# Hybrid decoder layer on 8 cores: where the first pieces, the row terms, the last quarter of x and the output blocks are loaded

## The reference

```python
proj = x @ w_in                       # 2048 x 10280: q, k, v, forget logits, z_att, z_ssd, xBC, dt
# 8 attention heads of 128: causal softmax(q k / sqrt(128) + F[t] - F[s]) v, F = cumsum(log sigmoid(f))
att = fox_attention(q, k, v, log_f) * silu(z_att)
# Mamba-2: conv of 4 taps and silu on xBC, 32 heads of 64 in 8 groups, chunks of 128
y = ssd_chunked(xs, dt, A, B, C) + d_skip * xs
y = gated_group_rmsnorm(y, z_ssd, ssd_norm_w)
x = layer_norm(2 ** 0.25 * x + concat([att, y]) @ w_out, ln_g, ln_b)
```

## Time and profile before

| | |
|---|---|
| Median of 3 runs | 1677.75 us |
| Profiled execution | 1675.15 us |
| Its span on the slowest core (core 1) | 1673.6 us |
| Spans of the 8 cores | 1664.3 to 1673.6 us |
| PE busy | 1635.6 us (98%) |
| DVE, POOL, ACT busy | 1135.5, 883.6, 849.6 us |
| DMA | 191.33 MB, mean 114 GB/s |

### The profile page before, as it was taken

The page is one execution under the profiler, slowest core; times in us unless marked ns, Lnnn a source line. Parts: engine busy times, 40 slices in busy tenths (PEclk is TensorE's granted clock), DMA queues, the critical chain, the costliest instruction groups (busy, mean ns, idle before and its releaser), DMA issues.

```text
span 1673.6 us, 31910 instructions; the slowest of 8 cores (1664.3 to 1673.6 us)
## 1 busy us (share of the span) xinstructions
PE 1635.6 (98%) x9108; PEld 801.4 (48%) x9108; DVE 1135.5 (68%) x2342; ACT 849.6 (51%) x1979; POOL 883.6 (53%) x1377
## 2 busy tenths in 40 slices
PE   5999999999999999999999999999999999999997
PEld 2454544544555455445554455455545544444443
DVE  2676777767876887678668876777778666444444
ACT  2767665665665666666666666666566610000000
POOL 2164564655664667468556765656567523222221
PEclk9999999999999999999999999999999999999999
DMA  9955954593457345644652473239556776445431
GB/s 169 149 79 92 134 97 93 114 123 91 104 103 131 81 92 110 112 97 85 126 87 73 89 139 64 54 77 157 110 112 126 197 194 189 138 139 139 139 95 76
DMA packets 180538, 191.33 MB, mean 114 GB/s; under 512 B 118828, under 2 KB 137132, under 8 KB 175980
## 3 DMA queue, kind: packets, MB, share of 16 engines
q1 hardware_dynamic: 164348, 126.89, 31.4%
q0 software_dynamic: 16016, 62.40, 23.5%
HBM read 198.74 MB, written 39.85 MB: 143 GB/s over the span
## 4 chain that ended last, share of the span: by engine, by line
PE 92%; DMA 4%; issue 1%; DVE 1%; ACT 1%; SPq 0%; POOL 0%; another core or an unknown queue 0%; DVEq 0%; ACTq 0%; POOLq 0%
PE bank L544 91%; DMA mixd<-att 1%; DMA xq<-xT 1%; DMA rowb<-arowd 1%; DMA mixd<-yn 1%; DMA xtok<-xsf 0%; SPq L603 0%; DVE xt L577 0%; PE bank L833 0%; ACT L555 0%; SPq L605 0%; PE bank L762 0%; ACT u L555 0%; ACT dec L555 0%; DVE acc L577 0%
## 5 line engine op out<-in xcount | busy, mean ns | idle before, releaser
L544 PE MATMUL bank<-xq,slab 128*128 128x512 bf16 x3072 | 726.0, 380 | 0.0
L544 PE MATMUL bank<-slab,xq 128*128 128x512 bf16 x2048 | 480.7, 379 | 1.1 <-DMA slab<-wpack 1.1
L544 PEld LDWEIGHTS bank<-xq,slab 128*128 128x128 bf16 x3072 | 293.9, 98 | 304.9 <-issue 3.9
L577 DVE SCALAR_TENSOR_TENSOR acc<-u,cst,acc 128x512 f32<-128x512 f32 x384 | 328.1, 857 | 51.5 <-ACT acc L555 38.8
L544 PEld LDWEIGHTS bank<-slab,xq 128*128 128x128 bf16 x2048 | 197.2, 98 | 211.4 <-issue 1.5
L555 ACT ACTIVATE dec<-rowb,nb 128x128 bf16<-128x128 f32 x512 | 202.2, 397 | 28.1 <-PE bank L544 16.2
L555 ACT ACTIVATE P<-bank,boff 128x512 bf16<-128x512 f32 x192 | 131.1, 683 | 68.7 <-PE bank L544 67.8
L544 PE MATMUL bank<-wo,mTa 128*128 128x512 bf16 x704 | 163.7, 379 | 0.0
L555 ACT ACT_TABLE_LOAD x14 | 18.0, 1283 | 273.6 <-DVE st L1169 270.3
L577 DVE SCALAR_TENSOR_TENSOR xt<-xt,bank 128x512 f32<-128x512 f32 x64 | 43.9, 685 | 141.1 <-PE bank L544 140.8
L566 POOL TENSOR_TENSOR xdd<-xtok,dtde 128x256 bf16<-128x256 bf16 x120 | 83.1, 692 | 85.3 <-PE bank L544 62.9
(11 more groups left out here) (113 smaller groups left out, 2197.8 us busy)
## 6 DMA issues: line engine op xcount, KB each, us to landing
slab<-wpack POOLq DMA_DIRECT2D x80, 512.0 KB, 8.7
rowb<-arowd SPq DMA_DIRECT2D x128, 256.0 KB, 4.0
xt<-x_tok SPq DMA_DIRECT2D x16, 1024.0 KB, 5.0
out<-xt SPq DMA_DIRECT2D x15, 1024.0 KB, 4.3
gbc<-growd SPq DMA_DIRECT2D x32, 256.0 KB, 5.2
mixd<-yn SPq DMA_DIRECT2D x128, 64.0 KB, 2.3
xq<-xT POOLq DMA_DIRECT2D x15, 512.0 KB, 33.8
wo<-w_out POOLq DMA_DIRECT2D x11, 512.0 KB, 9.6
```

The lines of the kernel that those rows point to most:

```text
L544: fns.append(lambda e, o=o, a=a, b=b, s=s, t=t: e.matmul(o, a, b, start=s, stop=t))
L577: return p.op("dve", [lambda e: e.scalar_tensor_tensor(out=o, in0=a, scalar=s, in1=b, op0=op0, op1=op1)], dve_us(n, nptr) + (0.12 if nptr ...
```

## The change

Four things. The first piece of x and the weights of `fdt` become casting loads at the head of POOL's stream, and the casts on ACT and DVE go. `copy_rows` goes, and all row loads read a single row. The last quarter of x is loaded behind k of step 1 instead of k of step 2, its `fdt` and `tab` are done within step 2 instead of step 3, the slots are used in turn, and the first three slabs of head 1 are loaded behind that `tab`. Blocks 3 to 13 of `w_out`, which go into the place of x, are loaded one by one, each behind a unit of steps 29 to 31.

```diff
-    queue = list(range(10)) + [0, 1, 2, 3, 4, 5, 6, 10, 11, 12, 7, 8, 9]
-    while len(queue) < 83:
-        queue.append(queue[-13])
+    queue = [n % 13 for n in range(83)]
...
+        if name == "fdt":
+            DMA("pool", [(fdtw[:, :], wpack[:, 0:1024])], "fdtw", [], [b_fdt], prio, 1 << 19)
...
-    DMA("sp", [(sf[:, :], wpack[:, 0:1024])], "sf", [], sfb, -3000, 1 << 19)
-    for h in range(2):
-        DMA("sp", [(sx[:, h * 1024:(h + 1) * 1024], xT[0, 0, :, h * 1024:(h + 1) * 1024])], "sx%d" % h, [],
-            [b_sx[h]] + (sxb if h == 0 else []), -2999 + h, 1 << 19)
...
-    stream = [(0, 1), "k", (0, 2), (0, 3), "xs0", "q", "xs1", (1, 0), (1, 1), (1, 2), (1, 3), "B", "C",
+    stream = ["fdt", (0, 0), (0, 1), "k", (0, 2), (0, 3), "xs0", "q", "xs1", (1, 0), (1, 1), (1, 2), (1, 3), "B", "C",
...
-    def copy_rows(q, t, gate):
-
-        qs = slice(q * 512, (q + 1) * 512)
-        a = arowd[:, 4 * q:4 * q + 4, :, :].rearrange("k c (g h) l -> (c g) k (h l)", h=4)
-        DMA("sp", [(growd[1:16, :, qs], growd[0:1, :, qs].to_broadcast([15, 8, 512])),
-                   (a[:, 1:16, :], a[:, 0:1, :].to_broadcast([32, 15, 512]))],
-            "rows%d" % q, [b_row1[q], gate], [b_row[q]], t, 1228800, 100.0)
...
-            DMA("sp", [(rb[:, :], arowd[ks, c, h4, :].rearrange("k h l -> k (h l)").unsqueeze(1).to_broadcast(
-                shape))], "rowb%d" % k3, [brow], [brb], t - 14, 262144, 200.0)
+            DMA("sp", [(rb[:, :], arowd[c:c + 1, h4, :].rearrange("k h l -> k (h l)").to_broadcast(
+                [128, 512]))], "rowb%d" % k3, [b_row1[q]], [brb], t - 14, 262144, 200.0)
...
+    def wo_load(n, prio, gate):
+
+        k = n - 2
+        home = at(xoff + k * 4096, [128, 2048], BF16, "wo")
+        late_home[n] = (home, b_xq[k // 4][k % 4])
+        DMA("pool", [(home[:, :], w_out[n])], "wo%d" % n, [], [b_xq[k // 4][k % 4]], prio, 1 << 20, after=gate)
+
...
-            if i == 0:
-                kinds = ["fdt"] + kinds[:4] + ["tab"] + kinds[4:]
+            if s == 2:
+                kinds = ["fdt", "k", "xs0", "q", "xs1", "tab", "fdt3", "tok0", "B", "tok1", "C", "tok2", "tab3", "tok3"]
...
+                if kind == "tab3":
+                    for n in (0, 1, 2):
+                        slab_load((KORD[n], 1), t + n)
                 if s == 2 and kind in ("k", "xs0", "q", "xs1"):
-                    x_load(3, ("k", "xs0", "q", "xs1").index(kind), t, [KT[2][1]])
+                    x_load(3, ("k", "xs0", "q", "xs1").index(kind), t, [KT[1][1]])
...
+                if s > 28:
+                    r = s % 2
+                    gates = {"k": KT[s % 5][1], "q": QT[r][1], "tok0": GZ[r][1], "tok1": GZ[r][1]}
+                    if kind in gates:
+                        n = 3 + 4 * (q - 1) + ("k", "q", "tok0", "tok1").index(kind) - 1
+                        if n >= 3:
+                            wo_load(n, t + 3, [gates[kind]])
...
-        if i == 1:
-            copy_rows(q, T[0] + 40, b_mix_att[1][q])
...
-    for n in range(1, 12):
-        homes.append((at(xoff + n * 4096, [128, 2048], BF16, "wo"), b_xq[n // 4][n % 4], start[28 + n // 4] + n % 4))
+    for n in range(3, 14):
+        homes.append(late_home[n] + (0.0,))
```

More of the change, by code:

```diff
@@ L510, in build_program @@
     fdtw = alloc([128, 1024], BF16, "fdtw")
-    b_fdt = [Buf("fdt%d" % h) for h in range(2)]
-    b_sx = [Buf("sx%d" % h) for h in range(2)]
-    b_x00 = [Buf("x00_%d" % n) for n in range(4)]
+    b_fdt = Buf("fdt")
     tokt = alloc([128, 4, 128], F32, "tokt")
@@ L625, in slab_load @@
     def slab_load(name, prio, gate=()):
[L626 to L630, removed]
+        if name == "fdt":
+            DMA("pool", [(fdtw[:, :], wpack[:, 0:1024])], "fdtw", [], [b_fdt], prio, 1 << 19)
+        else:
+            s = slot_of(*name)
+            o = woffs[name]
+            DMA("pool", [(slots[s][:, :], wpack[:, o:o + 2048])], "slot%d" % s, list(gate), [b_slot[s]], prio,
+                1 << 20, 300.0 if prio < -990 or name[1] > 1 else 230.0, after=pro_bufs if s >= NSLOT else ())
+            where[name] = s
     def x_load(q, j, prio, gate=()):
@@ L657, in build_program @@
             slab_load((it, 0), n - 1000)
[L659 to L660 removed]
+    DMA("sp", [(idn[:, :], cpack[:, 200:456])], "idn", [b_xq[0][0]], [b_idn], 0, 131072)
+    DMA("sp", [(rst[:, :], cpack[0:64, coffs["rst"][0]:coffs["rst"][0] + 512])], "rst", [b_xq[0][0]], [b_rst], 0, 131072)
     CPY("dve", idb[:, :], idn[:, 0:128], 128, [b_idn], [b_idb], 0)
@@ L743, in prologue_quarter @@
         qs = slice(q * 512, (q + 1) * 512)
-        DMA("sp", [(growd[0, :, qs], cs[0:8, :]),
-                   (arowd[0, 4 * q:4 * q + 4, :, :].rearrange("c p l -> p c l"),
+        DMA("sp", [(growd[:, qs], cs[0:8, :]),
+                   (arowd[4 * q:4 * q + 4, :, :].rearrange("c p l -> p c l"),
                     cs[32:64, :].rearrange("p (c l) -> p c l", c=4))], "row%d" % q, [bc], [b_row1[q]], pr, 81920, 30.0)
@@ L895, in attention @@
         gb, bgb = GBC[r]
-        ks, shape, brow = copies(i, g)
-        DMA("sp", [(gb[:, :], growd[ks, i, g * 512:(g + 1) * 512].unsqueeze(1).to_broadcast(shape))], "gbc%d" % r, [brow],
+        DMA("sp", [(gb[:, :], growd[i:i + 1, g * 512:(g + 1) * 512].to_broadcast([128, 512]))], "gbc%d" % r, [b_row1[g]],
             [bgb], base - 20, 262144, 200.0)
@@ L1068, in build_program @@
             for kind in kinds:
-                t = due() if kind != "tab" else T[0]
-                do_unit(kind, s, i, q, t)
+                t = T[0] if kind in ("tab", "tab3") else due()
+                if kind in ("fdt3", "tab3"):
+                    do_unit(kind[:3], s, i, 3, t)
+                else:
+                    do_unit(kind, s, i, q, t)
+                if kind == "tab3":
+                    for n in (0, 1, 2):
+                        slab_load((KORD[n], 1), t + n)
                 if s == 2 and kind in ("k", "xs0", "q", "xs1"):
-                    x_load(3, ("k", "xs0", "q", "xs1").index(kind), t, [KT[2][1]])
-                if s == 3 and kind in FM:
-                    slab_load((kind, 1), t)
-                elif q == 3 and 0 < i < 7 and kind in FM:
+                    x_load(3, ("k", "xs0", "q", "xs1").index(kind), t, [KT[1][1]])
+                if q == 3 and i < 7 and kind in FM:
                     slab_load((KORD[KORD.index(kind) + 3], i + 1), t + 3)
@@ L1080, in build_program @@
                         slab_load((KORD[n], i + 1), t, [GZ[s % 2][1]])
+                if s > 28:
[5 more added lines that the diff above has]
+                            wo_load(n, t + 3, [gates[kind]])
             T[0] += 4.5
-            if s == 3:
-                for n in (6, 7, 8, 9):
-                    slab_load((KORD[n], 1), T[0])
-            elif q == 3 and i < 7:
+            if q == 3 and i < 7:
                 slab_load((KORD[9], i + 1), T[0])
@@ L1108, in build_program @@
     for kb, (ap, buf, pr) in enumerate(homes):
-        if kb < 14:
+        if kb < 3:
             DMA("pool", [(ap[:, :], w_out[kb])], "wo%d" % kb, [], [buf], pr, 1 << 20)
-        else:
+        elif kb >= 14:
             DMA("sp", [(ap[:, :], wob[kb - 14])], "wo%d" % kb, [b_wob[kb - 14]], [buf], pr, 1 << 19)
@@ L1130, in load_mix @@
         ma, mb, bm = mtr[t % 3]
-        first = [pro_bufs + b_x00, conv_bufs, conv_bufs][t] if t < 3 else []
+        first = [pro_bufs + [b_xq[0][0]], conv_bufs, conv_bufs][t] if t < 3 else []
         ts = slice(t * 128, (t + 1) * 128)
```

38 lines of the change are left out of this document (11 added, 27 removed).

## The result

The changed kernel took 1693.02 us in the median of five runs (1689.74 us the fastest), the kernel before, beside it on the same chip, 1679.61 us: a ratio of 1.0087, with a 95% interval from 1.0063 to 1.0111. By the ratio 14.6 us are lost, and the time is outside the range of the prediction (1670 to 1688). A second measurement gave 1.0065 [1.0040, 1.0090].

A forecast was written before the change was run, and what follows sets the result against it. PE was taken as the bound, with little to win. Terms +1.8 - 2.1 + 0 + 0 + 0 = -0.3 us on 1675.15 gave 1674.85, and with the runs' median 2.6 us higher 1677.5; range 1670 to 1688.

The forecast's parts named there:

- What bounds the kernel: Whole kernel: PE busy 1635.6 of 1673.6 us, its waits only 27.0 us; 2% is about what a measurement can tell.
- the price of the row loads: Row loads of every step: single-row reads take 0.4 us more for 96 loads, hidden by three tiles in flight; sum 0.
- Rival (b): Heads 2 to 7: single-row loads come late beside slab loads, 2.9 us per head, +17.4 us, 1695 us; chance 0.12.
- Its threshold: POOL's row selection in heads 2 to 7: late rows decide once a load takes more than about 6.4 us.
- The copies' removal: SP's queue near 390 us: without copying DMAs the transposes no longer stand behind a wait, -2.1 us, at worst 0.
- Rival (c): Near 390 us: transposes wait for their inputs even without copies, so the gap stays, 1679.6 us; chance 0.05.
- The head: Start of POOL's stream: casting loads for the first pieces make later slabs land +1.8 us later; other end -1.7.
- rival (a): Start of the kernel: POOL's queue moves first bytes at 2.5 us, the head gains 1.7, 1674 us; chance 0.13.
- Last quarter sooner: x's last quarter and gates, loaded a step sooner: no PE wait, 0, with clumped slab loads between -2.9 and +2.9 us.
- output blocks: Steps 29 to 31, blocks loaded one by one on POOL: the last lands before PE needs it, 0, at most +1.5 us.

## Why the prediction was wrong

- What bounds the kernel held: PE, with little to win and all risk in new waits. That a measurement can hardly tell 2% from no change did not hold: the result's interval is 0.24% to either side, and its 0.87% is clear of that.
- **The step that failed** is the price of the row loads: "0.4 us more for 96 loads. That is hidden: three row tiles are in flight", with the sum 0. The 0.4 us was the difference of idle moments (3.4 to 3.7 against 3.1 to 3.2). Beside slab loads the median landing went to 6.0 us and single ones to 16.2, and three tiles in flight do not cover that. The row that said so was in hand, single-row loads of 3.7 to 10.8 us beside slabs, and of 16.1 to 24.7; I dismissed it because PE waited for none of those between 303 and 355 us. One stretch without harm was no bound for six heads.
- Rival (b) had the mechanism, but was given a chance of 0.12. That its time nearly agrees (1695 us for 1693.02) is luck. The price was not 2.9 us in each of six heads; it was up to three stalls of 2 to 7 us in a core, at places that differ between cores and executions, the longer ones with a piece at the lower clock behind them, and some of them behind a transpose and not a row. Its mark, POOL waiting 10 us for a row, is there at 839 us. Its threshold does not decide: before, 9 to 14 row loads a core took over 6.4 us between 400 and 1300 us and PE waited for none; after, 21 to 39 did. The mark for "wrong altogether", over 10 us of PE's waits between 100 and 400 us, stayed silent, since the loss lies behind 400 us.
- The copies' removal did what it said in the changed kernel: no core has a wait of PE between 375 and 400 us, where the earlier trace rows had 2.06 us. Rival (c) fell there. In the kernel before without copies the transposes were late all the same (1.1 to 4.1 us near 375 us on six cores), so this term hangs on the order.
- The head: the argument failed and the size held, by luck. POOL's queue starts early, as rival (a) had it and the Trainium skill, page "DMA: Bandwidth & Descriptors", section Specifications (about 1 us to the first byte from GpSimd's queue). Issued at 1.54 us, its first packet starts at 3.0 to 3.1 us on all cores, some 1.5 us later; the page's figure is nearer to that than to the 4.4 us and more of before. But x's first piece is there at 10.4 us (core 0), 7.4 us behind that start, where the prediction gave the two first pieces 5.0. In the mean of the cores the slabs land 0.1 to 0.5 us later than before up to 36 us, and 1.7 to 3.5 us later from 55 us on. PE did 103 matmuls fewer over eight cores in the first 100 us, 13 a core, at some 0.2 us each 2.6 us (the term was +1.8). By 375 us nothing of that is left. So rival (a)'s 1674 us did not come either.
- Last quarter sooner and output blocks, both put at 0: measured alone, 1.0009 and 0.9998, no difference clear of noise.
- The parts do not add. Reading alone cost 14 us, casts alone 17.6, and both with the rest 14.6, because stalls sit at single narrow places and the slowest core counts once. The prediction summed terms; for a kernel with an order of this kind that is right for work, not for waits.

What is not shown: why packets that read one row take longer, and how late rows come to make transposes late. The run with four copies was to tell whether the number of readers per row decides, and changed the number of engines with it. The second measurement of the changed kernel is smaller (1.0065, the intervals overlap); stalls that hit single cores in part of the executions make the median itself uneven.

## What to carry to other kernels

A load's price is to be read where it will run: beside the bulk loads, not in an idle moment, and one stretch in which late loads did no harm is not a bound for the others. Copies of a much-read row look like waste (4.9 MB here) and were worth 11 to 15 us in three orders that were kept fixed, but where they are made matters as much: kernels with them in other places came out 8 to 37 us over the one before. To test a cause in a kernel whose order is planned, keep the planner's numbers and change only what an instruction reads; experiments that let the order move mostly measured the new order's own narrow places.

## What the runs showed of the hardware

- Reading one 2 KB row 128 times in place of 16 copies 8 times raised the engine time of SP's queue from 24.6% to 33.7% at about equal bytes (50.66 and 48.59 MB), from 450 to 1350 us on core 3. The mean 2 KB packet of that queue took 0.11 to 0.12 us with 16 copies and 0.14 to 0.17 with one row, in the order of the kernel before.
- An access whose outermost dimension is four used four engines (12 x 120 completion packets missing), and the run with 120 such loads of 256 KB was some 30 us longer.
- With stores of 16 copies from 8 and 32 partitions PE stood for 31 to 35 us at 66 us.
- Around waits of PE of 8.5 and 5.5 us the granted clock fell: 0.62 and 0.66 in the windows that hold the wait's end, and 0.83 in one behind the second in which PE was busy throughout (the two levels mixed). Behind waits of 2 to 3 us it stayed at 1.00.
- SP's queue can be held at the issue itself: a row load's issue took 4.65 us and a transpose's 8.59 behind two copying transfers, where 0.54 and 1.22 are the medians of that run. Without copies near by the longest issues were 2.45 and 6.31 us (the changed kernel).
